# A Conformer encoder trunk: 31 depthwise taps on VectorE alone, and the first pointwise projection in full fp32

## The reference, cut to what matters

```python
def conformer_conv(h, pw1_w, pw1_b, dw_w, dw_b, ln_w, ln_b, pw2_w, pw2_b):
    u = h @ pw1_w + pw1_b                 # 256x2048 @ 2048x4096
    a, gate = jnp.split(u, 2, axis=-1)
    u = a * jax.nn.sigmoid(gate)
    u = depthwise_conv(u, dw_w) + dw_b    # width 31, centred
    u = jax.nn.silu(layernorm(u, ln_w, ln_b))
    return u @ pw2_w + pw2_b              # 256x2048 @ 2048x2048
```

## Time and profile before

| | us |
|---|---|
| median of 3 runs | 3431.38 |
| lowest and highest of them | 3426.4, 3434.28 |
| the profiled execution | 3434.32 |
| its span in the trace | 3432.7 |

### The profile page before, as it was taken

How to read it: one execution, slowest core, us unless ns; L and a number is a source line. 1 busy time by engine, 2 the same in 40 slices (tenths; PEclk the granted TensorE clock), 3 DMA queues, 4 the chain that set the end, 5 groups by cost and what they waited for, 6 DMA issues and landing times.

```text
span 3432.7 us, 38330 instructions
## 1 busy us (share of the span) xinstructions
PE 2947.0 (86%) x13702; PEld 2444.6 (71%) x13702; DVE 2428.1 (71%) x2215; ACT 1395.4 (41%) x1371; POOL 374.5 (11%) x318
## 2 busy tenths in 40 slices
PE   1699999987777698999999999766538899999998
PEld 1577778866666577788888888655427788888886
DVE  7588868866766477887787776589975655555555
ACT  0256634334554334433333333544434433333333
POOL 0011111233333000000000000033420000000000
PEclk9899999999999799999999999988769999999998
DMA  9466766663332598787898887433215666666663
GB/s 363 183 221 228 252 217 207 223 227 101 95 95 62 175 358 333 273 333 296 309 339 326 310 304 261 139 100 98 86 37 171 233 206 199 211 205 206 202 213 122
DMA packets 322143, 731.27 MB, mean 213 GB/s; under 512 B 48128, under 2 KB 64336, under 8 KB 293648
## 3 DMA queue, kind: packets, MB, share of 16 engines
q1 hardware_dynamic: 316256, 709.85, 58.7%
q0 software_dynamic: 5808, 20.35, 1.8%
HBM read 710.45 MB, written 19.69 MB: 213 GB/s over the span
## 4 chain that ended last, share of the span: by engine, by line
PE 73%; DVE 14%; issue 4%; ACT 4%; DMA 3%; SPq 1%; DVEq 1%; POOL 0%; ACTq 0%; POOLq 0%
PE psg L631 44%; PE psg L637 22%; DVE y L1501 5%; DMA aring<-in_ada_w 2%; PE psn L658 1%; DVE exb L1350 1%; ACT dec L1775 1%; PE pst L797 1%; PE pst L620 1%; DVE wlo L1018 1%; DVE lm L1314 1%; DVE aacc L1114 1%; DMA wraw<-in_gdn_out_w 1%; PE psn L620 1%; PE pst L790 1%
## 5 line engine op out<-in xcount | busy, mean ns | idle before, releaser
L1584 ACT ACTIVATE whi<-wraw 128x2048 fp32r<-128x2048 f32 x441 | 844.7, 1916 | 1399.5 <-PE psg L637 1319.5
L1018 DVE TENSOR_TENSOR wlo<-wraw,whi 128x2048 fp32r<-128x2048 f32 x441 | 1012.7, 2297 | 517.3 <-ACT whi L1584 515.4
L631 PE MATMUL psg<-whi,h_hi 128*128 128x512 f32 (+1 forms) x2592 | 824.7, 400 | 36.8 <-DVE h_lo L1544 13.0
L631 PE MATMUL psg<-whi,h_lo 128*128 128x512 f32 (+1 forms) x2592 | 812.0, 395 | 0.0
L637 PE MATMUL psg<-wlo,h_hi 128*128 128x512 f32 (+1 forms) x2592 | 662.3, 400 | 102.5 <-DVE wlo L1018 102.3
L637 PEld LDWEIGHTS psg<-wlo,h_hi 128*128 128x128 f32 x2592 | 499.8, 195 | 212.0 <-DVE wlo L1018 108.7
L631 PEld LDWEIGHTS psg<-whi,h_hi 128*128 128x128 f32 x2592 | 495.3, 194 | 142.3 <-issue 22.4
L631 PEld LDWEIGHTS psg<-whi,h_lo 128*128 128x128 f32 x2592 | 498.5, 193 | 105.0
L1028 DVE SCALAR_TENSOR_TENSOR aacc<-aring,cond,aacc 128x2048 f32<-128x2048 f32 x151 | 354.3, 2346 | 8.3 <-DMA aring<-in_ada_w 7.9
L631 PE MATMUL psg<-whi,g_hi 128*128 128x512 f32 x704 | 219.9, 394 | 0.0
L631 PE MATMUL psg<-whi,g_lo 128*128 128x512 f32 x704 | 219.2, 393 | 0.0
(11 more groups left out here) (216 smaller groups left out, 2686.8 us busy)
## 6 DMA issues: line engine op xcount, KB each, us to landing
aring<-in_ada_w SPq DMA_DIRECT2D x192, 1024.0 KB, 6.9
wraw<-in_ffn_in_w SPq DMA_DIRECT2D x176, 1024.0 KB, 6.8
wraw<-in_gdn_in_w SPq DMA_DIRECT2D x97, 1024.0 KB, 5.2
wraw<-in_ffn_out_w SPq DMA_DIRECT2D x88, 1024.0 KB, 5.3
wraw<-in_cf_pw_w SPq DMA_DIRECT2D x48, 1024.0 KB, 5.3
wraw<-in_gdn_out_w SPq DMA_DIRECT2D x32, 1024.0 KB, 8.5
wraw<-d_rr SPq DMA_DIRECT2D x16, 1024.0 KB, 5.3
x<-in_x SPq DMA_DIRECT2D x2, 2048.0 KB, 9.6
```

What stands on the lines that cost most here:

```text
L631: mm(ps[:, t, 0:width], a[:, kc, t * P:(t + 1) * P], wh, start=first and j + n == 0, stop=False)
L1018: tt(wlo[:, j % 2, :], wraw[:, j % 4, :], whi[:, j % 2, :].bitcast(F32), SUB).then_inc(w_lo, 1)
L1584: av(whi[:, j % 2, :], wraw[:, j % 4, :], ACT.Copy).then_inc(w_hi, 1)
```

## The change

**Taps.** `TAPS_V` now holds all 31 taps. `products`, the rings `dwp` and `dwa`, GpSimd's loop and the closing addition are gone. The last `stt` of a slice raises `dw_ok` itself. Each of the four instructions of a tap now has a wait of its own, for the instruction four places before it (the same block of the tap before), and its own count on `tap`.

**Projection.** `tile32` does 8 fp32 matmuls for each tile, straight from `wraw` against the unsplit activations `h32`, which lie in `aring3`. There is no `hi` and no `lo` for these 32 tiles. SP's loads from the fifth on wait for `w_used` in place of `w_lo`. `pre(2)` writes `h32` and has no split. Counts after the stage are shifted by 32 (`unsplit`).

```diff
-TAPS_S = tuple(range(6)) + tuple(range(CTAPS - 6, CTAPS))
-TAPS_V = (CTAPS // 2,) + tuple(k for k in range(6, CTAPS - 6) if k != CTAPS // 2)
+TAPS_V = (CTAPS // 2,) + tuple(k for k in range(CTAPS) if k != CTAPS // 2)
...
+                if raw:
+                    sp.wait_ge(w_used, g - 3)
+                elif not isinstance(g, int) or g >= 4:
+                    sp.wait_ge(w_lo, g - 3 - unsplit)
...
+            def tile32(g, slot, ps, a, kcs, first, last, ready):
+
+                pe.wait_ge(w_land[slot], 4 * (g - slot) + 16)
+                pe.wait_ge(*ready)
+                for j, kc in enumerate(kcs):
+                    for t in range(TT):
+                        i = mm(ps[:, t, :], a[:, kc, t * P:(t + 1) * P], wraw[:, slot, j * NSL:(j + 1) * NSL],
+                               start=first and j == 0, stop=last and j == len(kcs) - 1)
+                i.then_inc(w_used, 1)
...
-                    tile(G_P1 + 8 * n + j, (G_P1 + j) % 2, psg[:, (S_P1 + j // 4) % 2], h_hi3, h_lo3,
-                         range(4 * (j % 4), 4 * (j % 4) + 4), j % 4 == 0, j % 4 == 3,
-                         ready=(pre_lo, 8 + j % 4 + 1))
+                    q = j % 4
+                    tile32(G_P1 + 8 * n + j, (G_P1 + j) % 4, psg[:, (S_P1 + j // 4) % 2], h32,
+                           range(4 * q, 4 * q + 4), q == 0, q == 3, ((hf_v, hf_s)[q % 2], 4 + q // 2 + 1))
...
-                    if m:
-                        dve.wait_ge(tap, dwt.at())
                     for b in range(4):
+                        if m:
+                            dve.wait_ge(tap, dwt.at() - 3)
...
-                    dwt.inc(i)
-                if part and part[-1][0] == len(TAPS_V) - 1:
-
-                    dve.wait_ge(tap, dwt.at())
-                    dve.wait_ge(dwa_ok, (len(TAPS_S) + 1) * (n + 1))
-                    dst = dwo[:, ds(4 * n, 4), :]
-                    tt(dst, dst, dwa, ADD).then_inc(dw_ok, 1)
-
-            def pw1_pair(n, lag):
-                for j in range(8):
-                    if lag or j >= 2:
-                        lo(G_P1 + 8 * n + j, G_P1 + j)
-                    if lag and j == 1:
-                        unit(n - 1)
-                    if lag and j >= 1:
-                        dw(n - 1, order[(j - 1) * 3:j * 3])
-            pw1_pair(0, False)
-            with dwt.loop(dve, 1, 4, len(TAPS_V)) as i:
-                pw1_pair(i, True)
+                        if m == CTAPS - 1 and b == 3:
+                            i.then_inc(dw_ok, 1)
+                        else:
+                            dwt.inc(i)
+
+            def pw1_pair(n):
+                unit(n - 1)
+                dw(n - 1, order)
+            with dwt.loop(dve, 1, 4, 4 * CTAPS - 1) as i:
+                pw1_pair(i)
...
-                if f == 0:
-                    hi(G_P1 + 1, G_P1 + 1)
```

More of the change, by code:

```diff
@@ L397, in _, with load_w @@
         def _(sp):
-            def load_w(g, slot, src, dst=None):
-                if not isinstance(g, int) or g >= 4:
-                    sp.wait_ge(w_lo, g - 3)
+            def load_w(g, slot, src, dst=None, unsplit=0, raw=False):
+                if raw:
+                    sp.wait_ge(w_used, g - 3)
+                elif not isinstance(g, int) or g >= 4:
+                    sp.wait_ge(w_lo, g - 3 - unsplit)
                 sp.dma_start(tile4(wraw[:, slot, :]) if dst is None else dst, src).then_inc(w_land[slot], 16)
@@ L590, in load_ffn @@
                     g = g0 + 8 + 12 * (GRP - 1) + j
-                    load_w(g, g % 4, rows4(w_out, (GRP - 1) * NSL, j * NSL))
+                    load_w(g, g % 4, rows4(w_out, (GRP - 1) * NSL, j * NSL), unsplit=skip)
             load_ffn(0, G_F0)
-            with sp.Fori(0, 4) as i:
+            for i in range(4):
                 for j in range(8):
-                    load_w(G_P1 + 8 * i + j, (G_P1 + j) % 4, rows4(pw1, (j % 4) * KT * P, i * NSL + (j // 4) * D))
+                    load_w(G_P1 + 8 * i + j, (G_P1 + j) % 4, rows4(pw1, (j % 4) * KT * P, i * NSL + (j // 4) * D),
+                           raw=8 * i + j >= 4)
             for j in range(4):
-                load_w(G_P2 + j, (G_P2 + j) % 4, rows4(pw2, j * KT * P, 0))
+                load_w(G_P2 + j, (G_P2 + j) % 4, rows4(pw2, j * KT * P, 0), raw=True)
             sp.wait_ge(t_g, 4)
@@ L1050, in pre @@
                 dve.wait_ge(aff_ok, n + 1)
+                if hi is None:
+                    for q in (0, 2):
+                        dve.wait_ge(pre_tr, 4 * n + q + 1)
+                        for j in range(4):
+                            kc = 4 * q + j
+                            i = ts(hfb[:, kc, :], pst[:, j, :], aff[:, n, kc:kc + 1], mod[:, 3 * n, kc:kc + 1], MUL, ADD)
+                        i.then_inc(hf_v, 1)
+                    return
                 def low(q):
                     dve.wait_ge((hf_v, hf_s)[q % 2], 2 * n + q // 2 + 1)
-                    dve.wait_ge(pre_hi, 4 * n + q + 1)
+                    dve.wait_ge(pre_hi, (0, 4, 8, 8)[n] + q + 1)
                     tt(lo_[:, 4 * q:4 * q + 4, :], hfb[:, q % 2], hi[:, 4 * q:4 * q + 4, :].bitcast(F32),
@@ L1468, in _ @@
             post(1, y, cwb)
-            pre(2, y, h_hi3, h_lo3, hf3, 11, 8, lambda: lo(G_P1 + 1, G_P1 + 1))
+            pre(2, y, None, None, h32, 11, 8)
+            unsplit[0] = 32
             cw_col(2, 11)
@@ L1567, in _ @@
             post(2, y, cwb)
-            pre(3, y, h_hi3, h_lo3, hf3, 11, 16, lambda: lo(G_F1 + 1, G_F1 + 1))
+            pre(3, y, h_hi3, h_lo3, hf3, 11, 12, lambda: lo(G_F1 + 1, G_F1 + 1))
             ffn(1, G_F1, S_F1)
@@ L1619, in odd @@
                     act.wait_ge(pre_tr, 4 * n + q + 1)
-                    if q == 3:
+                    if q == 3 and hi_ is not None:
                         act.wait_ge(pre_lo, low0 + 2)
@@ L1896, in _ @@
             squares(2, lambda t: (x_up, 3 + t))
-            pre(2, h_hi3, hf3, 8)
+            pre(2, None, h32, 8)
             def half(n, which):
@@ L1911, in sigm @@
                 i.then_inc(sg_ok, 1)
-            def products(n, part):
-                act.wait_ge(glu_ok, n + 1)
-                for m in part:
-                    k = TAPS_S[m]
-                    off = k - CTAPS // 2
-                    a, e = max(0, -off), T - max(0, off)
-                    act.wait_ge(dwa_ok, (len(TAPS_S) + 1) * n + max(0, m - 2))
-                    for b in range(4):
-                        i = av(dwp[:, m % 4, b, a:e], glu[:, b, a + off:e + off], ACT.Copy,
-                               scale=vec[:, ds(NV_DW + k * KC + 4 * n + b, 1)])
-                    i.then_inc(dwp_ok, 1)
             def pw1_pair(n, lag):
@@ L1932, in pw1_pair @@
                         half(n, 0)
-                    if lag or j >= 2:
-                        hi(G_P1 + 8 * n + j, G_P1 + j)
                     if lag and j == 2:
                         sigm(n - 1)
-                    if lag and j >= 2:
-                        products(n - 1, range(2 * j - 4, 2 * j - 2))
             pw1_pair(0, False)
@@ L1943, in _ @@
             sigm(3)
-            products(3, range(len(TAPS_S)))
             hi(G_P2, G_P2)
@@ L1975, in _ @@
             squares(3, lambda t: (x_up, 5 + t))
-            pre(3, h_hi3, hf3, 16)
+            pre(3, h_hi3, hf3, 12)
             ffn(1, G_F1, S_F1)
```

48 lines of the change are left out of this document (18 added, 30 removed).

## The result

| | before | changed |
|---|---|---|
| median of the runs, us | 3428.9 (4 runs, 3425.8 to 3434.3) | 3349.2 (4 runs, 3340.9 to 3356.0) |
| profiled execution, us | 3434.3 | 3356.0 |
| ratio | | 0.9765, 95% interval 0.9738 to 0.9792 |

The change makes the kernel 2.35% faster. The forecast was 3356 with a range of 3346 to 3372.

A forecast was written before the change was run, and what follows sets the result against it. VectorE was taken as the bound from 2230 us on, slowed by GpSimd's additions. The first LayerNorm sum moves from 2532.3 to 2456.4, 75.9 us less: 3434.3 becomes 3358.4, the median 2.9 lower, 3355.5 (called 3356); range 3346 to 3372.

The forecast's parts named there:

- Head of the stage: Before the first projection: without ScalarE's weight copy and the h_lo wait, the first tile starts 2.4 us earlier, at 2174.6.
- A tile in fp32: First projection on TensorE: 16 records of 0.43 us, 6.88 us a tile, 1.44 more than in fp32r.
- rival C: First projection: fp32 weight loads are not hidden, a tile costs 8.61 us, about 3409 us in all; chance 0.05.
- The chains: TensorE done at 2401.0; VectorE's slice 2 starts at 2355.2, slice 3 at 2406.0 and ends at 2456.3.
- The removal of the contention: VectorE's taps: the slow ones (7.61 us against 1.65) lie beside GpSimd additions; without these nothing holds them.
- Rivals A and B: A: taps keep 1.81/1.70 us steps, 13 us later, chance 0.15; B: every wait blocks like direct-predecessor, about 3443 us, chance 0.04.
- Behind it: After the last tap: closing addition of 1.24 us goes, LayerNorm sum starts at 2456.4, later stages unchanged within 3 us.
- The median: Whole kernel: profiled execution forecast at 3358.4 us, median 2.9 us below it, 3355.5 us.

The follow-up runs named there:

- the run with additions: Changed kernel plus 12 GpSimd additions of 128x1024 per slice on a scratch tile, whose result nobody uses; 3442.8 us, ratio 1.0035.
- the run with taps only: Kernel before with all 31 taps on VectorE and the waits four places back, projection kept in fp32r with its split; 3394.1 us, ratio 0.990.
- the run with half of the projection: Changed kernel with two of four contraction chunks of each first-projection tile left out, all transfers kept; 3317.2 us, ratio 0.967.

## Why the prediction was right

*Head of the stage.* Update of `x` forecast for 2157.6, seen at 2157.53; first tile forecast for 2174.6, seen at 2174.2. The multiplication behind the removed copy was indeed what is late next. That the absolute times agree to tenths is luck: in other executions with the same code up to here the first tile starts between 2162.6 and 2177.2 us. The differences are what counts, 2.4 us forecast for the head and 2.9 seen.

*A tile in fp32.* 0.43 us a record forecast, 0.429 seen over 512 records, with only the transposes between them. The unhidden weight load (rival C) isn't there: L630's weight loads lie beside the matmul in front. Nor is the pace that the four passes of the Trainium skill ("FP8 and Floating Point Precision", TensorE Precision Notes) would give at the fp32r step (0.227 a pass): two records of 0.429 make 0.86, not 0.91. This doesn't speak against the four passes, which would be 0.215 us each; it was the fp32r step that didn't fit. The rows of another line, same operation and width, were the right source for the price.

*The chains.* TensorE's end was forecast at 2401.0 and seen at 2400.2; slice 2 at 2355.2, seen 2354.5; slice 3 at 2406.0, seen 2404.5; the last sum's start at 2456.4, seen 2454.1. Of these last 2.3 us, 1.2 are the tap instruction (0.388 us for 0.393, 120 times, twice on the chain) and 0.7 the earlier start of slice 2; the rest is `unit` and the centre tap and rounding. TensorE and VectorE reach slice 3 nearly together, as the sum had it. VectorE's idle time in front of `unit` was to be 5 to 6 us and is 6.8.

*The removal of the contention.* Argued from the earlier trace rows by coincidence in time; the run with additions shows it as cause.

*Rivals A and B.* Both mechanisms are real and cost what was said (13.3 us for 13; 99 for 88 to 90, of which 5.7 are the gaps where the loop goes round), but they belong to other distances of the wait. The argument that decided, that a wait four places back is long satisfied, held.

*Behind it.* From the first sum to the first `h_lo` 27.2 us passed before and 27.2 after, and from there to the end of the span 873.3 and 873.2, so that the bound of 3 us for the clock wasn't needed in the profiled execution.

*The median.* The 3356 is the profiled execution's forecast less 2.9 us. The profiled execution came 2.4 us below its forecast (3356.0 for 3358.4), but it was the slowest of four: the median is 3349.2, 6.8 us below the profiled one, where I had allowed 2.9. So the median lies 6.3 us under the 3355.5, of which 2.4 are the sum and 3.9 the spread between launches; the ratio was forecast as 0.978 and is 0.9765.

*What wasn't foreseen.* Not in the prediction, but in the expectations: the handover in the run with taps only (16 to 20 us missing), the late landing with the low clock behind it (7 us) and the gaps where the loop goes round (4 us) in the run with half of the projection, the sums behind TensorE's taps (3 us). Most of them are the same mistake, a sum of the bound engine's work without the chain between engines at its borders. The prediction's own sum had these steps in it and came out.

## What to carry to other kernels

Moving work off a helper engine can pay even when the engine that takes it is the bound: here 12 additions on GpSimd cost VectorE 23 to 25 us a slice, more than the 12 taps that it took over (48 x 0.39 = 19 us). When an engine accumulates in place in short instructions, put independent ones between two that depend on each other and wait for exactly the one needed. And once the bound has moved, look at the stretches where the old bound idles (here pair 0 and the tail behind the last tile): the two together gave another 34 us of the stretch, 2.9 of which come back in the head.

## What the runs showed of the hardware that I had not expected

- A `ts` of 128x256 in fp32 with both operands in SBUF takes 0.41 us alone and 2.14 to 2.40 us beside GpSimd memsets, which an `stt` with two inputs doesn't notice.
- A wait on an instruction that is long complete costs VectorE nothing that shows, even with two register instructions for each of 0.388 us; a wait on the direct predecessor costs 0.26 us in a loop with register counts and 0.12 with constants (21 instructions in 10.62 us).
- In the run with half of the projection the first loads of the stage took 14.8 us to land (median of four) where the earlier trace rows have 5.3. TensorE idled 3.92 us for them, and its granted clock was 0.56 in the 6 us behind that.
- Depthwise taps as fp32 matmuls with a diagonal run at 0.45 us for up to 128x256 (two records of 0.225 in the mean, at a granted clock of 0.94), against 0.39 us on VectorE: TensorE is a fair second engine for them when it idles, with ScalarE writing a diagonal in 0.30 us.
